# Gated linear attention: both key halves of a distance in one TensorE visit, next operands scaled a step later, outputs by kind

## The reference

```python
def gla_chunk_step(S, inp):
    qc, kc, vc, ac = inp
    b = jnp.cumsum(ac, axis=2)
    decay = jnp.exp(-jnp.abs(b[:, :, :, None, :] - b[:, :, None, :, :]))
    scores = jnp.einsum('bhtk,bhsk,bhtsk->bhts', qc, kc, decay)
    o = jnp.einsum('bhts,bhsv->bhtv', scores, vc) + jnp.einsum('bhtk,bhkv->bhtv', qc * jnp.exp(b), S)
    b_end = b[:, :, -1:, :]
    S_new = jnp.exp(b_end[:, :, 0, :])[..., None] * S + jnp.einsum('bhsk,bhsv->bhkv', kc * jnp.exp(b_end - b), vc)
    return S_new, o
```

## Time and profile before

| what | value |
|---|---|
| median of 3 runs | 1402.03 us (1400.67 to 1404.07) |
| the profiled execution's own time | 1401.66 us |
| its span, first to last instruction | 1399.9 us |
| PE busy | 1392.9 us, 99% of the span |
| DVE, ACT, POOL busy | 922.7, 594.8, 211.4 us |
| granted TensorE clock | 1.0 of full speed over the whole span |

### The profile page before, as it was taken

One profiled execution on the slowest core, in us unless ns is written; L12 is line 12 of the kernel. 1 busy time (PEld: TensorE's weight loads), 2 busy tenths in 40 slices (PEclk: granted clock), 3 DMA queues, 4 the chain that ended last, 5 costly groups with the idle time before them and its releaser, 6 DMA issues.

```text
span 1399.9 us, 21738 instructions
## 1 busy us (share of the span) xinstructions
PE 1392.9 (99%) x8714; PEld 1185.3 (85%) x8714; DVE 922.7 (66%) x1264; ACT 594.8 (42%) x842; POOL 211.4 (15%) x214
## 2 busy tenths in 40 slices
PE   9999999999999999999999999999999999999998
PEld 7898889777888989889888997778888998989886
DVE  6645433766767759587656678656756857758775
ACT  5324531554444445353243435344434535344353
POOL 5000000000022302112332020000022221303310
PEclk9999999999999999999999999999999999999999
DMA  5224223211336936635332322232225764827573
GB/s 184 91 91 114 61 68 100 75 55 41 117 106 151 212 104 164 165 97 143 113 98 75 91 69 76 83 96 78 91 94 150 174 159 113 213 90 198 132 177 109
DMA packets 154861, 161.62 MB, mean 115 GB/s; under 512 B 4010, under 2 KB 144660, under 8 KB 154788
## 3 DMA queue, kind: packets, MB, share of 16 engines
q1 hardware_dynamic: 122868, 129.12, 29.2%
q0 software_dynamic: 31904, 31.46, 12.4%
q10 hardware_dynamic: 16, 0.00, 0.0%
HBM read 157.68 MB, written 2.10 MB: 114 GB/s over the span
## 4 chain that ended last, share of the span: by engine, by line
PE 99%; ACT 0%; DVE 0%; issue 0%; POOL 0%; POOLq 0%; ACTq 0%
PE ps L2359 63%; PE ps L2424 17%; PE ps L2355 4%; PE ps L2381 4%; PE ps L2497 3%; PE ps L2751 1%; PE ps L2567 1%; PE ps L2778 1%; PE ps L2869 1%; PE ps L2764 1%; PE ps L2656 0%; PE ps L2544 0%; PE ps L2951 0%; PE ps L2699 0%; PE ps L2717 0%; PE ps L2663 0%
## 5 line engine op out<-in xcount | busy, mean ns | idle before, releaser
L2359 PE MATMUL ps<-AA,wh 128*128 128x512 f32 x1440 | 454.0, 397 | 0.0
L2359 PE MATMUL ps<-BB,wh 128*128 128x512 f32 x1088 | 342.2, 396 | 0.2 <-issue 0.2
L2359 PEld LDWEIGHTS ps<-AA,wh 128*128 128x128 f32 x1440 | 267.3, 188 | 69.7 <-issue 6.9
L2359 PE MATMUL ps<-AA,wl 128*128 128x512 f32 x720 | 283.3, 394 | 0.0
L917 ACT ACTIVATE wh<-raw 128x1024 fp32r<-128x1024 f32 (+2 forms) x149 | 141.5, 950 | 261.7 <-PE ps L2359 207.9
L2359 PEld LDWEIGHTS ps<-BB,wh 128*128 128x128 f32 x1088 | 202.2, 188 | 49.5 <-issue 1.8
L2359 PE MATMUL ps<-BB,wl 128*128 128x512 f32 x544 | 213.9, 393 | 0.0
L1451 DVE TENSOR_TENSOR wl<-raw,wh 128x1024 fp32r<-128x1024 f32 (+2 forms) x149 | 170.0, 1141 | 60.6 <-ACT wh L917 60.3
L2359 PEld LDWEIGHTS ps<-AA,wl 128*128 128x128 f32 x720 | 135.4, 188 | 30.9
L2359 PEld LDWEIGHTS ps<-BB,wl 128*128 128x128 f32 x544 | 102.3, 188 | 23.3
L2424 PE MATMUL ps<-Hl,wh 128*128 128x256 f32 x384 | 107.8, 281 | 0.0
(11 more groups left out here) (404 smaller groups left out, 2405.3 us busy)
## 6 DMA issues: line engine op xcount, KB each, us to landing
raw<-in_w_in SPq DMA_DIRECT2D x38, 1024.0 KB, 5.4
raw<-in_w_ff SPq DMA_DIRECT2D x31, 1024.0 KB, 5.4
raw<-in_w_mlp_in SPq DMA_DIRECT2D x16, 1024.0 KB, 5.5
raw<-in_w_mlp_out SPq DMA_DIRECT2D x16, 1024.0 KB, 5.3
zf<-in_w_mlp_out POOLq DMA_DIRECT2D x48, 256.0 KB, 4.6
zf<-in_w_ff POOLq DMA_DIRECT2D x48, 256.0 KB, 4.8
raw<-in_w_out SPq DMA_DIRECT2D x8, 1024.0 KB, 5.1
arena<-in_x SPq DMA_DIRECT2D x4, 512.0 KB, 6.1
```

The lines of the kernel that those rows point to most:

```text
L2359: last = pe.matmul(dense_psum(t_ps, kind), a[:, k, :], b[:, o0 + k, col0:col0 + S1], start=start, stop=stop)
```

## The change

Units y and y+1 of one level are now handled together: `unit_qk` of both stands in the even step y+2, ahead of that step's own `unit_d`, and `unit_mm` of both in the odd step y+3. Before, `unit_qk` of unit y stood in step y+1 behind the `unit_d` of that step. This holds for units 0 to 13; units 14 to 17 stay where they were. The second unit of a pair writes the upper half of the same PSUM banks, DVE waits for the visit of both, and `o_mm` now makes all 16 score products (both halves i, one head after the other), waits once, and then all 16 state products, with the two heads alternating.

```diff
-    units = 2 * (len(LEVELS) + 3)
+    units, paired = 2 * (len(LEVELS) + 3), 2 * (len(LEVELS) + 1)
     t = T2_A
     for y in range(units + 2):
+        if y % 2 == 0 and 0 <= y - 2 < paired:
+            between[t] += [("unit_qk", y - 2), ("unit_qk", y - 1)]
         if y < units:
             between[t] += [("unit_d", y)]
-        if 0 <= y - 1 < units:
+        if paired <= y - 1 < units:
             between[t] += [("unit_qk", y - 1)]
-        if 0 <= y - 2 < units:
+        if y % 2 and 0 <= y - 3 < paired:
+            between[t] += [("unit_mm", y - 3), ("unit_mm", y - 2)]
+        if paired <= y - 2 < units:
             between[t] += [("unit_mm", y - 2)]
...
-                    act.wait_ge(o_step, 8 * j + 8)
+                    act.wait_ge(o_step, 3 * j + 3)
...
-                    dve.wait_ge(mm_done, y + 1)
-                    src = ps[:, 4:6, 0:4 * CH]
+                    dve.wait_ge(mm_done, 2 * l + 2)
+                    src = ps[:, 4:6, j * 4 * CH:(j + 1) * 4 * CH]
...
-                    if y >= 1:
-                        pe.wait_ge(sc_done, min(y, U_END))
+                    if y >= 2:
+                        pe.wait_ge(sc_done, min(y - j, U_END))
...
-                                mm = pe.matmul(ps[parity_rows(r), 4 + hh, i * CH:(i + 1) * CH],
+                                mm = pe.matmul(ps[parity_rows(r), 4 + hh, (4 * j + i) * CH:(4 * j + i + 1) * CH],
...
-                    for i in range(2):
-                        quads = [(4 * q + 2 * i + r, q, r) for r in range(2) for q in range(2)]
-                        for hh in range(2):
-                            h = 2 * j + hh
-                            if i == 1:
-                                pe.wait_ge(o_step, 8 * j + 3 + hh)
-                            for c, q, r in quads:
...
+                    chunks = [(4 * q + 2 * i + r, i, q, r) for i in range(2) for r in range(2) for q in range(2)]
+                    for hh in range(2):
+                        h = 2 * j + hh
+                        for c, i, q, r in chunks:
...
+                                           start=(i == 0), stop=False, skip_group_check=True)
+                        mm.then_inc(o_step, 1)
+                    pe.wait_ge(o_step, 3 * j + 2)
+                    for c, i, q, r in chunks:
                         for hh in range(2):
...
```

More of the change, by code:

```diff
@@ new lines, in job @@
+                    for hh in range(2):
+                        h = 2 * j + hh
+                        for c, i, q, r in chunks:
+                            rows = parity_rows(r)
+                            mm = pe.matmul(ps[CH * q:CH * q + CH, 4 + 2 * hh + r, i * P:(i + 1) * P],
+                                           sc[rows, j, hh * 4 * CH + c // 2 * CH:hh * 4 * CH + (c // 2 + 1) * CH],
+                                           Vn[rows, (c + 1) // 2, h * P:(h + 1) * P],
+                                           start=(i == 0), stop=False, skip_group_check=True)
+                        mm.then_inc(o_step, 1)
@@ L2918, in job @@
-                            mm.then_inc(o_step, 1)
+                            mm = pe.matmul(ps[CH * q:CH * q + CH, 4 + 2 * hh + r, i * P:(i + 1) * P],
+                                           Qs[b:b + 64, j, c * CH:(c + 1) * CH],
+                                           st[b:b + 64, j, c * P:(c + 1) * P],
+                                           start=False, stop=True, skip_group_check=True)
+                    mm.then_inc(o_step, 1)
                 elif kind == "o_scale":
```

## The result

The changed kernel takes 1406.38 us in the median (1404.47 to 1406.63, 8 runs), the kernel before in the same comparison 1401.43 us (1400.67 to 1404.07, 8 runs). The forecast was 1404.6 us with a range of 1400.8 to 1408.0. The profiled execution after took 1406.47 us, with a span of 1404.7 us against 1399.9 before.

A forecast was written before the change was run, and what follows sets the result against it. PE was taken to bound the kernel, its chain lying there for 99% of the span. From 1401.66 us, 3.1 saved (2.4 visits, 0.7 outputs) and 6.0 of new waits (5.8 rounded up) gave 1404.6, range 1400.8 to 1408.0.

The forecast's parts named there:

- Visits, 2.4 us saved: PE's visits between slab matmuls: 14 become 7, the second unit costing 0.47 instead of 0.81 us, 2.4 us saved.
- Outputs, 0.7 us saved: PE's outputs: alternating heads give state products the score products' pace, 0.36 us saved per j, 0.7 in all.
- Its upper bound: Most the outputs could save: 1.5 us, with the state products at half of 0.54.
- Waits at slabs 6, 8, 10 and 12: PE's new waits for DVE's `wl` at these slabs: 1.5, 2.3, 1.2 and 0.8 us, 5.8 in sum.
- slab 4 had none, as said: At slab 4, fed by step 2, the prediction gave PE no wait, with a bound of 0.9 us.
- Slab 10's 1.2: PE's wait at slab 10, from step 8: `wl` done at 847.31 against PE's arrival at 846.14, 1.2 us.
- Slab 12's 0.8: PE's wait at slab 12, from lateness passed through steps 10 and 11: between 0 and 1.6, taken as 0.8 us.
- Slab 6's sum: PE's wait at slab 6: `wl` at 819.0 against 817.83, 1.2 us, up to 1.9, taken as 1.5.
- Slab 8's wait: PE's wait at slab 8, from step 6: 1.6 us, up to 2.5 if POOL interferes, taken as 2.3.
- one more DVE operation meets POOL: In step 6, ahead of slab 8: a further DVE operation overlaps POOL's sums, raising the wait from 1.6 to 2.5 us.
- waits without POOL: Rival, chance 0.2: POOL's sums miss DVE's scalings, slabs 6, 8, 10, 12 wait 0, 1.6, 1.2, 0.8 us; 1402.2 us.
- lateness is carried on: Rival, chance 0.15: slab 4 waits 0.9 us, slabs 6 and 8 0.86 more each, giving 1407.2 us.

The follow-up runs named there:

- experiment 5: The kernel before with only the new order of the outputs: 1401.16 us, ratio 0.9995 to the kernel before.
- experiment 6: The changed kernel with the outputs' state products taken eight of one head, then eight of the other, instead of alternating: 1406.42 us in one execution.
- experiment 4: The changed kernel with POOL's window sums of the third and fourth pooled group cut to 16 columns: 1402.41 us, ratio 1.0003 to the kernel before.
- experiment 8: The changed kernel run once more, unaltered: 1406.73 us, ratio 1.0036 to the kernel before.
- experiment 3: The kernel before with only the scalings of both units moved ahead of the even step's difference, visits still single: 1421.16 us, ratio 1.0126.

## Why the prediction was right, point by point

- **Visits, 2.4 us saved: right.** The changed kernel makes 7 visits of 64 instructions, their first to last start 1.16 - 0.22 = 0.94 us apart (0.95 foretold), where 32 took 0.47: the second unit costs 0.47 each time.
- **Outputs, 0.7 us saved: right in the sum and in the reason, its parts by luck.** 0.37 for each j (0.36 foretold); experiment 5 has it alone, experiment 6 shows that the alternation is the reason. But the state products save 0.72 + 0.80 - 1.04 = 0.48, more than the 0.36, and the score products with the one full wait behind them take 0.11 back (1.19 against 2 x 0.54), where the prediction put nothing; the two errors cancel. Its upper bound was also short: with the state products at half of 0.54 it is 4 x (0.72 - 0.27) = 1.8, not 1.5; the forecast does not rest on it. The sixteen state products start within 0.83 us when key rows alternate and 1.32 when they don't. The Trainium skill, TensorEngine Tiling (Array Packing), Key Properties, says that different tiles can load weights and multiply in parallel; here products on the same key rows, in two different quarters, went slower than products on different ones, and the upper bound that the prediction drew from that rule was not reached.
- **Waits at slabs 6, 8, 10 and 12, each for `wl`, DVE for `wh`, ACT for the difference: right**, in the place, the releaser and the order. Taken were 1.5, 2.3, 1.2 and 0.8, measured 1.69, 2.81, 1.25 and 0.89; slab 4 had none, as said. Slab 10's 1.2 was worked out from rows and came true. Slab 12's 0.8 was the middle of 0 to 1.6, so that it is near is luck. Slab 6's sum gave 1.2 and was raised to 1.5 for another reason; what it lacked is that two pairs of visits lie ahead of slab 6, not one, so that PE came 0.66 earlier (817.51, counted as above, against 818.17) and not 0.34, while `wl` was done at 819.15, near the 819.0 foretold.
- **Slab 8's wait was sized too low**, 2.3 against 2.81 and above its bound of 2.5. The order's part is smaller than its 1.6 (1.43 in experiment 4), so POOL's was the mis-sized one: "one more DVE operation meets POOL" was counted at 0.86 at the most, one fixed block, but the scaling that met it lost 1.78 - 0.68 = 1.10, nearly all that was left of POOL's add, and without POOL slab 8's wait is shorter by 1.38 in all.
- **The rival "waits without POOL" is what experiment 4 measured:** foretold 0, 1.6, 1.2 and 0.8 us of waits and 1402.2 us, found 0, 1.43, 1.25 and 0.89 and 1402.41. It did not come about in the changed kernel since the overlap is there, as argued.
- **What the sum left out is the clock.** With the measured waits it is -2.4 - 0.74 + 6.64 = +3.5 us; the fall of the clock adds 1.5, together 5.0, and the spans differ by 1404.7 - 1399.9 = 4.8. Without the fall the two executions of the first comparison lie at 1404.47 and 1404.67, on the forecast of 1404.6; in the median the forecast is 1.8 too low. The prediction priced the waits by their own length and did not ask what PE would do behind them. That the median is nearer to the 1407.2 of the rival "lateness is carried on" is no sign for that rival: slab 4 did not wait, and slab 6 waited 0.2 longer than taken, not 0.86.

What stays open: in which executions the clock falls behind slab 8's wait, and why in some it stays down longer, no run here tells. The length of the wait alone does not decide it: 2.74 us was followed by a fall in the profiles of the changed kernel and of experiment 8, but not in that of experiment 6, and 1.82 us was in experiment 3.

## What to carry to other kernels

When work is moved so that two of a kind come together, look for the one short instruction that now stands behind both and for the engine that waits on it; here putting the difference back ahead of the scalings, at the price of two buffers, turned +0.31% into -0.13%. Price a wait of the bounding engine at its length and then ask for its clock behind it. A part that saves by itself (here the outputs) can be below what a comparison of medians tells, and still be read from the timeline.

## What the runs showed of the hardware

- A wait of 2.7 us by TensorE in the midst of a stretch that was otherwise busy was followed by the lower clock in 10 of 14 executions, as their mean clock tells; in the two of them that were profiled it was granted 0.53 over 3.5 us, which cost 1.5 us, and 0.50 to 0.71 over 7.8 us, which cost 2.8. Waits of 1.6 us and 1.2 us in the same executions were not followed by a fall; in experiment 3 one of 1.82 us was, and one of 0.97 was not.
- A DVE operation that met POOL's sums grew by up to 1.10 us, from 0.68 to 1.78. It grew by 0.85 with 0.98 us left of POOL's add and by 1.10 with 1.23 left, so the cost goes with what is left of POOL's instruction and is not one fixed block.
- Sixteen fp32 products of 64 rows (32 instructions) start within 0.83 us when neighbours use different key rows, and within 1.32 us when eight in a row use the same ones.
